# A seven-product group for the third row group of the first two down-projection blocks, in three of the four quarters of both MLPs

## The chip, the cores and the metric

The kernel runs on one core of one Trainium2 chip. The metric is the device time of one execution in microseconds (us); lower is better. Before the change the median of three runs is 1988.44 us (1988.22 to 1989.09).

## What is computed

A decoder trunk of two layers on 256 tokens (two tiles of 128) with a stream of width 2048, all in float32: differential attention and an MLP, then a shared latent K/V, latent attention and a second MLP. The change touches the MLPs alone. Their width is 8192:

```
def sq_relu_mlp(h, w_up, w_down):
    return jnp.square(jax.nn.relu(h @ w_up)) @ w_down
...
        x = x + sq_relu_mlp(rms_norm(x, mlp_norm_g[l]), w_up[l], w_down[l])
```

## The kernel before

**Three products for one.** Every float32 product is made of three: an operand is split into a high part (rounded to the format in which TensorE multiplies) and a low part (the rest), and high x high, high x low and low x high are summed in PSUM. Activations are split once (`opA` holds the normalised input, `opB` the hidden activations). Weights are split as they stream in: SyncE loads quads of 512 rows x 512 columns (4 chunks of 128 rows, 1 MB) into the four slots of `raw`, ScalarE copies two chunks at a time to `whi` (`split` of ScalarE, L1080), VectorE subtracts the copy from `raw` into `wlo` (`split` of VectorE, L1672), and TensorE runs the twelve 512-column matmuls of these two chunks (`half_tok`, L595 to L597: 2 chunks x 2 token tiles x 3). Such a piece is called a half here; a quad has two, a block of 2048 rows x 512 columns eight. `whi` and `wlo` are rings of four halves: ScalarE may write a half when TensorE has done the one four places earlier, so VectorE can be at most some four halves ahead.

**The MLP.** The hidden width is worked in four quarters of 2048 (`QUARTERS`). In a quarter the up-projection makes four hidden blocks of 512 columns (j = 0 to 3), each squared, turned (a transpose of 32x32 blocks on VectorE, four DMAs from `o_sb` to `prob` by SyncE's `move_quads`) and split into `opB`. Then the down-projection multiplies them by four column blocks of `w_down` (j = 0 to 3), each with four row groups r = 0 to 3 of 512 rows; row group r needs hidden block r. Blocks 0 and 1 are `first_down`, blocks 2 and 3 are `pair` (in the last quarter: plain blocks). TensorE's order in `first_down` is `DOWN_ORDER`, pairs (j, r), so that the last hidden block is used late:

```
DOWN_ORDER = ((0, 0), (0, 1), (0, 2), (1, 0), (0, 3), (1, 1), (1, 2), (1, 3))
```

**Seven products instead of eight.** Two quads of the same rows in two column blocks, times two token tiles, make a 2x2 by 2x2 product of blocks (256 rows x 512 columns x 128 tokens each). Plain, it costs four halves, 48 matmuls. `seven` makes it of seven products of six matmuls (L828 to L830), 42 in all, in the order `FORMS`: B22, T1, B21, B11, T2, T3, T4. It needs sums of activations (`form_sums`, `form_low` of VectorE; `form_high` of ScalarE), four sums of weights (VectorE, L2199, L2202, L2209, L2213), and each of the seven weight operands split on its own: four through the ring (L2188), three (T1, B11, T3) through `extra_hi`/`extra_lo` (L2182), which has two places, so T3 may be written only when TensorE has done T1 of the same group. Four of the products go to more than one output: they are summed in four PSUM banks of their own (`side`), copied out by ScalarE, mixed by four VectorE operations (`combine`, L2105), and added to the outputs. The up-projection uses one group per pair of blocks, `pair` two (row groups 2 and 3), which share the `side` banks, one copy and one `combine`. `down_add` (L2251, two operations of 128x1024) adds the mixed shares of `pair` to the residual stream `xs`, inside the group of the next up-projection (`up_pair`, after its first weight sum). `add_scaled` (L2136) adds the accumulators.

VectorE's and ScalarE's orders are written out by hand: `body`, `pair` and `up_pair` say after which split which other step comes. Each engine executes in its own order.

## Time and profile before

| | us |
|---|---|
| median of three runs | 1988.44 |
| the profiled execution, its own time | 1988.36 |
| its span, first to last instruction | 1986.6 |
| TensorE matmuls busy | 1977.4 (9128 matmuls) |
| TensorE weight loads busy | 1651.8 |
| VectorE busy | 1582.4 |
| ScalarE busy | 1161.1 |
| DMA, mean rate | 204 GB/s |

The chain of work that ended last is TensorE for 97% of the span and VectorE for 1%. Matmuls are pipelined: the recorded length of one (0.39 us) overlaps the next, and what counts is the distance between two starts. The same holds for VectorE, whose records of 1.22 us start 1.14 us apart when nothing is waited for. A bracket at the end of a timeline row is idle time of the engine before the instruction, and what ended it.

### The profile page before, as it was taken

What the parts mean: (1) busy time and instruction counts of PE and PEld (TensorE: products, weight loads), DVE (VectorE), ACT (ScalarE), POOL (GpSimd) and SP (SyncE); (2) the same over time, 40 slices, a digit from 0 to 9 for tenths busy, and PEclk for the clock granted to TensorE, in tenths of its full rate; (3) what the DMA queues carried; (4) which work ended last, traced back from release to release, by engine and by line L of the source; (5) the groups of instructions that cost most, each with busy time, mean ns of one, the idle gap of its engine ahead of it and who ended that gap; (6) DMA issues with size and microseconds to landing.
All of it is one profiled execution on the core that took longest, in us unless ns stands there. A gap on an engine that the chain in (4) does not pass through costs nothing.

```text
span 1986.6 us, 24882 instructions
## 1 busy us (share of the span) xinstructions
PE 1977.4 (100%) x9128; PEld 1651.8 (83%) x9128; DVE 1582.4 (80%) x1931; ACT 1161.1 (58%) x1481; POOL 13.2 (1%) x21
## 2 busy tenths in 40 slices
PE   9999999999999999999999999999999999999998
PEld 8888888888888888888888998888888888888887
DVE  7789996678888798788866787667798788889865
ACT  6555555556566456556656665556456556655653
POOL 0000000000000000000000000000000000000000
PEclk9999999999999999999999999999999999999999
DMA  8655546666566557656766554676557656656663
GB/s 307 212 170 189 182 157 216 225 194 234 190 215 223 191 200 241 220 190 202 242 212 195 143 152 151 223 229 223 181 194 240 223 199 212 227 186 212 212 240 106
DMA packets 265924, 405.26 MB, mean 204 GB/s; under 512 B 18416, under 2 KB 88432, under 8 KB 265840
## 3 DMA queue, kind: packets, MB, share of 16 engines
q1 hardware_dynamic: 251920, 395.82, 60.0%
q10 hardware_dynamic: 13920, 8.39, 1.5%
q8 instruction: 44, 0.72, 0.1%
q14 instruction: 40, 0.33, 0.0%
HBM read 379.00 MB, written 2.10 MB: 192 GB/s over the span
## 4 chain that ended last, share of the span: by engine, by line
PE 97%; issue 2%; DVE 1%; ACT 0%; POOL 0%; POOLq 0%; DVEq 0%; ACTq 0%
PE acc L595 24%; PE acc L597 24%; PE acc L596 24%; PE side L829 2%; PE side L830 2%; PE side L828 2%; PE acc L828 2%; PE acc L830 2%; PE acc L615 2%; PE acc L616 2%; PE acc L617 2%; PE acc L829 2%; PE acc L933 1%; PE acc L934 1%; PE acc L935 1%
## 5 line engine op out<-in xcount | busy, mean ns | idle before, releaser
L1672 DVE TENSOR_TENSOR wlo<-raw,whi 128x1024 fp32r<-128x1024 f32 (+1 forms) x596 | 709.7, 1206 | 214.7 <-ACT whi L1080 212.8
L1080 ACT ACTIVATE whi<-raw 128x1024 fp32r<-128x1024 f32 (+1 forms) x596 | 614.0, 1046 | 431.6 <-PE acc L597 360.4
L595 PE MATMUL acc<-whi,opB 128*128 128x512 f32 x1104 | 431.2, 391 | 0.1
L597 PE MATMUL acc<-whi,opB 128*128 128x512 f32 x1104 | 430.1, 390 | 0.0
L596 PE MATMUL acc<-wlo,opB 128*128 128x512 f32 x1104 | 429.9, 389 | 0.0
L595 PE MATMUL acc<-whi,opA 128*128 128x512 f32 (+2 forms) x1072 | 415.0, 387 | 0.0
L597 PE MATMUL acc<-whi,opA 128*128 128x512 f32 (+2 forms) x1072 | 414.2, 386 | 0.0
L596 PE MATMUL acc<-wlo,opA 128*128 128x512 f32 (+2 forms) x1072 | 414.1, 386 | 0.0
L597 PEld LDWEIGHTS acc<-whi,opB 128*128 128x128 f32 x1104 | 207.3, 188 | 43.2
L595 PEld LDWEIGHTS acc<-whi,opB 128*128 128x128 f32 x1104 | 207.4, 188 | 42.7 <-DVE wlo L1672 0.3
L596 PEld LDWEIGHTS acc<-wlo,opB 128*128 128x128 f32 x1104 | 207.4, 188 | 42.5
L597 PEld LDWEIGHTS acc<-whi,opA 128*128 128x128 f32 x1072 | 201.4, 188 | 40.0
L596 PEld LDWEIGHTS acc<-wlo,opA 128*128 128x128 f32 x1072 | 201.5, 188 | 39.8
L595 PEld LDWEIGHTS acc<-whi,opA 128*128 128x128 f32 x1072 | 201.5, 188 | 39.8
L1405 ACT ACTIVATE whi<-raw 128x1024 fp32r<-128x1024 f32 x78 | 82.9, 1063 | 96.5 <-DVE raw L2209 49.0
L1401 ACT ACTIVATE extra_hi<-raw 128x1024 fp32r<-128x1024 f32 x52 | 54.7, 1052 | 84.0 <-PE side L830 84.0
L2188 DVE TENSOR_TENSOR wlo<-raw,whi 128x1024 fp32r<-128x1024 f32 x78 | 95.1, 1219 | 0.0
L2182 DVE TENSOR_TENSOR extra_lo<-raw,extra_hi 128x1024 fp32r<-128x1024 f32 x52 | 63.6, 1222 | 23.1 <-ACT extra_hi L1401 23.1
L2087 DVE STREAM_TRANSPOSE o_sb<-junk 128x1024 f32<-128x1024 f32 x32 | 39.8, 1243 | 44.8 <-ACT junk L1359 44.8
L615 PE MATMUL acc<-whi,opA 128*128 128x512 f32 x184 | 72.0, 391 | 0.3 <-DVE wlo L1672 0.2
L616 PE MATMUL acc<-wlo,opA 128*128 128x512 f32 x184 | 71.7, 390 | 0.0
L617 PE MATMUL acc<-whi,opA 128*128 128x512 f32 x184 | 71.7, 389 | 0.0
(379 smaller groups left out, 2383.3 us busy)
## 6 DMA issues: line engine op xcount, KB each, us to landing
raw<-in_w_up SPq DMA_DIRECT2D x128, 1024.0 KB, 5.5
raw<-in_w_down SPq DMA_DIRECT2D x128, 1024.0 KB, 5.1
raw<-in_a_w_qkv SPq DMA_DIRECT2D x44, 1024.0 KB, 5.1
raw<-in_a_w_o SPq DMA_DIRECT2D x16, 1024.0 KB, 5.1
prob<-o_sb SPq DMA_DIRECT2D x128, 128.0 KB, 2.6
raw<-in_b_w_o SPq DMA_DIRECT2D x16, 1024.0 KB, 5.0
raw<-in_w_ukv SPq DMA_DIRECT2D x32, 256.0 KB, 4.2
prob<-o_sb ACTq DMA_DIRECT2D x48, 128.0 KB, 4.3
```

The lines of the kernel that those rows point to most:

```text
L595: mm(o, a_hi, w_hi, start=start, stop=False)
L596: mm(o, a_hi, w_lo, start=False, stop=False)
L597: done = mm(o, a_lo, w_hi, start=False, stop=last and c == chunks - 1)
L615: mm(o, a_hi, whi[:, place, :], start=start, stop=False)
L616: mm(o, a_hi, wlo[:, place, :], start=False, stop=False)
L617: done = mm(o, a_lo, whi[:, place, :], start=False, stop=end)
L828: mm(o, a_hi, hi[:, place + c, :], start=first and c == 0, stop=False)
L829: mm(o, a_hi, lo[:, place + c, :], start=False, stop=False)
L1080: done = fn(whi[:, place:place + ch, 0:n], raw[:, r, c0:c0 + ch, 0:n], ACT.Copy)
L1405: fn(whi[:, 2 * (hf % 4):2 * (hf % 4) + 2, :], source[f], ACT.Copy).then_inc(hi_ready, 1)
L1672: done = tt_(wlo[:, place:place + ch, 0:n], raw[:, r, c0:c0 + ch, 0:n], whi[:, place:place + ch, 0:n].bitcast(F32), ALU.subtract)
L2188: tt_(wlo[:, places, :], src, whi[:, places, :].bitcast(F32), ALU.subtract).then_inc(lo_ready, 1)
```

## The change

In quarters 0 to 2 of both MLPs row group 2 of down blocks 0 and 1 becomes a seven-product group of its own kind, "first". TensorE's order in `first_down` is now (0,0), (0,1), (1,0), (1,1), the group, (0,3), (1,3). Its four shares are copied by ScalarE at the end of `first_down`, combined by VectorE in `pair` between the two groups there, and added to `xs[:, :, 0:1024]` by a `down_add` in `pair`. The combine and `down_add` of `pair`'s own shares move on into the next `up_pair`. The activation sums for row group 2 are made straight from the turned hidden block (no more rebuilt from `opB`), so that the move of the next hidden block waits for them. TensorE's hardware loop over the quarters is written out. What only renumbers groups, shares and places is left out:

```diff
-DOWN_ORDER = ((0, 0), (0, 1), (0, 2), (1, 0), (0, 3), (1, 1), (1, 2), (1, 3))
+DOWN_FIRST = ((0, 0), (0, 1), (1, 0), (1, 1))
+DOWN_LAST = ((0, 3), (1, 3))
+LAST_DOWN = ((0, 0), (0, 1), (0, 2), (1, 0), (0, 3), (1, 1), (1, 2), (1, 3))
...
+def groups_of(l):
+
+    made = [("up", l, 0, 1)]
+    for q in range(QUARTERS - 1):
+        made += [("first", l, q), ("down", l, q, 0), ("down", l, q, 1), ("up", l, q + 1, 0), ("up", l, q + 1, 1)]
+    return made
...
@@ SyncE @@
+                    if j == JB - 1 and q < QUARTERS - 1:
+                        sp.wait_ge(form_step, 4 * (FORM_SETS * l + 2 * q + 1) + 4)
...
-                    for k, (j, r) in enumerate(DOWN_ORDER):
+                    order = DOWN_FIRST + ((0, 2), (1, 2)) + DOWN_LAST
+                    if q == QUARTERS - 1:
+                        order = LAST_DOWN
+                    for k, (j, r) in enumerate(order):
...
-                        quad(b + i // 4, i % 4, src, later=int(i == 6))
+                        quad(b + i // 4, i % 4, src, later=int(i in (0, 6)))
...
@@ TensorE @@
+                    for k, (j, r) in enumerate(DOWN_FIRST):
+                        plain_quad(k, j, r)
+                    pe.wait_ge(hid_lo, n + 6)
+                    shares_free(SHARE["first", l, q])
+                    pe.wait_ge(form_lo, FORM_SETS * l + 2 * q + 2)
+                    seven(GROUP["first", l, q], b + 1, 0, opB, 8, [forms[0][:, i] for i in range(2)], None, True, SHARED)
+                    for k, (j, r) in enumerate(DOWN_LAST):
+                        plain_quad(6 + k, j, r)
 
-                with pe.Fori(0, QUARTERS - 1) as q:
+                for q in range(QUARTERS - 1):
                     first_down(q)
...
@@ ScalarE @@
+                def copy_shared():
+                    for k in range(4):
+                        fn(down_shared[k], side[k], ACT.Copy).then_inc(shared_copied, 1)
...
+                def first_down(q):
+
+                    b = B_MLP[l] + 2 * JB * q + JB
+                    split(b, 3)
+                    square_second(q, 1)
+                    split(b, 4)
+                    hid_high(q, JB - 2)
+                    split(b, 5)
+                    split(b, 6)
+                    down_forms(q, 0)
+                    split(b, 7)
+                    seven(GROUP["first", l, q], b + 1, 0, (0, b + 1), (1, b + 1), {"B11": lambda: hid_high(q, JB - 1)})
+                    for hf in range(4, 8):
+                        split(b + 1, hf)
+                        if hf == 5:
+                            down_forms(q, 1)
+                    copy_shared()
+                    for hf in range(3):
+                        split(b + 2, hf)
...
                     split(b + 2, 0)
                     split(b + 2, 1)
-                    for k in range(4):
-                        fn(down_shared[k], side[k], ACT.Copy).then_inc(shared_copied, 1)
+                    act.wait_ge(shared_added, 2 * DOWN_SHARE["first", l, q] + 2)
+                    copy_shared()
                     split(b + 2, 2)
...
@@ VectorE @@
+                def down_add(key, c0):
+
+                    dve.wait_ge(shared_sums, 4 * SHARE[key] + 4)
+                    for s in range(2):
+                        dve.wait_ge(drained[s], 2 * (u[s] + U_QUARTER * key[2] + U_UP + c0 // 2 + 1))
+                    for t, both in enumerate((junk[:].rearrange("p a n -> p (a n)"), o_sb[:].rearrange("p a t n -> p (a t n)"))):
+                        stt(out=xs[:, t, NB * c0:NB * c0 + 2 * NB], in0=both, scalar=rs[:, 2 * l + 1, t:t + 1],
+                            in1=xs[:, t, NB * c0:NB * c0 + 2 * NB], op0=ALU.mult, op1=ALU.add).then_inc(shared_added, 1)
+
+                def first_down(q):
+
+                    b, key = B_MLP[l] + 2 * JB * q + JB, ("first", l, q)
+                    uses = [u[s] + U_QUARTER * q + U_UP for s in range(2)]
+                    split(b, 3)
+                    up_turn(q, JB - 1)
+                    split(b, 4)
+                    hid_low(q, JB - 2)
+                    form_sums(sqT, down_set(q, 0))
+                    split(b, 5)
+
+                    def after_first():
+                        split(b, 6)
+                        form_low(down_form(0), down_set(q, 0))
+
+                    seven(GROUP[key], b + 1, 0, (0, b + 1), (1, b + 1), 8 * b + 3,
+                          {"first sum": after_first, "second sum": lambda: split(b, 7), "B11": lambda: hid_low(q, JB - 1)})
...
-                    seven(down_groups(l, q, 0), 1, b, 4, (2, b), (3, b), 8 * b + 3, {"first sum": lambda: split(b, 3)})
+                    seven(GROUP["down", l, q, 0], b, 4, (2, b), (3, b), 8 * b + 3, {"first sum": lambda: split(b, 3)})
+                    combine(SHARE["first", l, q], down_shared)
                     split(b + 1, 0)
-                    seven(down_groups(l, q, 1), 2, b + 1, 2, (1, b + 1), (2, b + 1), 8 * b + 8,
+                    seven(GROUP["down", l, q, 1], b + 1, 2, (1, b + 1), (2, b + 1), 8 * b + 8,
                           {"first sum": lambda: split(b + 1, 1)})
                     split(b + 1, 6)
+                    down_add(("first", l, q), 0)
                     split(b + 1, 7)
...
                     for hf in range(3):
                         split(b + 2, hf)
-                    combine(down_shares(l, q), down_shared)
                     add_scaled(b + 1, 0, 2 * uses[0], slice(3 * NB, 4 * NB))
...
                         if follows == "down":
-                            down_add(q - 1)
+                            combine(SHARE["down", l, q - 1, 0], down_shared)
...
-                    if follows != "down":
+                    if follows == "down":
+                        after["T4"] = lambda: down_add(("down", l, q - 1, 0), 2)
+                    else:
                         after["T4"] = lambda: hid_low(q, 2 * i - 1)
```

**How the order moves.** Three places on VectorE. The first is `pair`, from T3 and T4 of its first group to the middle of its second. Before (L2182 and L2188 are the low parts of a group, L1672 that of a plain half, L2199, L2202, L2209, L2213 the weight sums):

```order
L2182 TENSOR_TENSOR extra_lo<-raw,extra_hi 128x1024
L2188 TENSOR_TENSOR wlo<-attn_both,whi 128x1024
L1672 TENSOR_TENSOR wlo<-raw,whi 128x1024
L2199 TENSOR_TENSOR attn_both<-raw 128x1024
L1672 TENSOR_TENSOR wlo<-raw,whi 128x1024
L2202 TENSOR_TENSOR raw<-raw 128x1024
L2188 TENSOR_TENSOR wlo<-raw,whi 128x1024
L2182 TENSOR_TENSOR extra_lo<-attn_both,extra_hi 128x1024
L2209 TENSOR_TENSOR raw<-attn_both,raw 128x1024
```

And with the change (L2211 and L2217 are the low parts of a group, L1705 that of a half, L2138 is `combine`):

```order
L2211 TENSOR_TENSOR extra_lo<-raw,extra_hi 128x1024
L2217 TENSOR_TENSOR wlo<-attn_both,whi 128x1024
L2138 TENSOR_TENSOR o_sb<-o_sb,junk 128x512
L2138 TENSOR_TENSOR junk<-junk,o_sb 128x512
L2138 TENSOR_TENSOR o_sb<-o_sb 128x512
L2138 TENSOR_TENSOR o_sb<-junk,o_sb 128x512
L1705 TENSOR_TENSOR wlo<-raw,whi 128x1024
L2228 TENSOR_TENSOR attn_both<-raw 128x1024
L1705 TENSOR_TENSOR wlo<-raw,whi 128x1024
L2231 TENSOR_TENSOR raw<-raw 128x1024
L2217 TENSOR_TENSOR wlo<-raw,whi 128x1024
```

Four operations have come in between the low part of T4 and that of the next half. The second place is `up_pair` after a `pair`, from T3 of its group on. Before:

```order
L2182 TENSOR_TENSOR extra_lo<-raw,extra_hi 128x1024
L2188 TENSOR_TENSOR wlo<-attn_both,whi 128x1024
L1672 TENSOR_TENSOR wlo<-raw,whi 128x1024 x4
L2105 TENSOR_TENSOR junk<-junk 128x512
L2105 TENSOR_TENSOR attn_both<-attn_both,junk 128x512
```

With the change (L2259 is `down_add`):

```order
L2211 TENSOR_TENSOR extra_lo<-raw,extra_hi 128x1024
L2217 TENSOR_TENSOR wlo<-attn_both,whi 128x1024
L2259 SCALAR_TENSOR_TENSOR xs<-junk,rs,xs 128x1024
L2259 SCALAR_TENSOR_TENSOR xs<-o_sb,rs,xs 128x1024
L1705 TENSOR_TENSOR wlo<-raw,whi 128x1024 x4
```

Two operations stand now ahead of the four halves that follow the group. The third place is the new group in `first_down`, with the change, from the low part of hidden block 2 on (L2128 is `hid_low`, L2180 to L2185 `form_sums`, L2190 `form_low`):

```order
L2128 TENSOR_TENSOR opB<-prob,opB 128x4x256
L2180 TENSOR_TENSOR qk_first<-prob 128x256
L2181 TENSOR_TENSOR qk_first<-prob 128x256
L2183 TENSOR_TENSOR qk_first<-prob,qk_first 128x256
L2185 TENSOR_TENSOR qk_first<-prob,qk_first 128x256
L1705 TENSOR_TENSOR wlo<-raw,whi 128x1024
L2228 TENSOR_TENSOR attn_both<-raw 128x1024
L1705 TENSOR_TENSOR wlo<-raw,whi 128x1024
L2190 TENSOR_TENSOR v_hl<-qk_first,v_hl 128x1024
L2231 TENSOR_TENSOR raw<-raw 128x1024
L1705 TENSOR_TENSOR wlo<-raw,whi 128x1024
L2217 TENSOR_TENSOR wlo<-raw,whi 128x1024
```

Before, three plain low parts stood behind the first of these rows, and the form sums came later.

## Rows read from the trace of the kernel before

**Rows 1.** The page: busy time of each engine.
```profile
PE 1977.4 (100%) x9128; PEld 1651.8 (83%) x9128; DVE 1582.4 (80%) x1931; ACT 1161.1 (58%) x1481; POOL 13.2 (1%) x21
```
**Rows 2.** The waits of TensorE: who released it, us, times, longest.
```profile
PE side L648 <- DVE junk L1827: 1.1, 1, 1.1
...
PE acc L615 <- DVE wlo L1672: 0.2, 1, 0.2
```
**Rows 3.** Stages first_down, pair: us; PE, PEld, DVE, ACT, POOL busy; granted clock, DMA.
```profile
465.60:509.13 43.53, 43.53 (x193) 36.05 (x192) 31.68 (x35) 23.83 (x23) 0.00 (x0) 1.00 0.66 220
509.13:552.99 43.86, 43.86 (x193) 36.02 (x192) 39.62 (x38) 25.23 (x27) 0.00 (x0) 1.00 0.61 203
```
**Rows 4.** Timeline, TensorE, that quarter: start us, us, line, operation.
```profile
509.13 0.39 PE L595 MATMUL acc<-whi,opB 128*128 128x512 f32 x1
...
520.02 0.40 PE L828 MATMUL acc<-whi,v_hl 128*128 128x512 f32 x1
...
529.75 0.39 PE L595 MATMUL acc<-whi,opB 128*128 128x512 f32 x1
...
539.39 0.39 PE L828 MATMUL side<-extra_hi,opB 128*128 128x512 f32 x1
...
576.45 0.39 PE L595 MATMUL acc<-whi,opA 128*128 128x512 f32 x1
```
**Rows 5.** Timeline, VectorE, pair: T3 and T4 of its first group onward.
```profile
524.17 1.23 DVE L2182 TENSOR_TENSOR extra_lo<-raw,extra_hi 128x1024 fp32r<-128x1024 f32 x1 [2.07 <-ACT extra_hi L1401]
525.31 1.22 DVE L2188 TENSOR_TENSOR wlo<-attn_both,whi 128x1024 fp32r<-128x1024 f32 x1
526.44 1.22 DVE L1672 TENSOR_TENSOR wlo<-raw,whi 128x1024 fp32r<-128x1024 f32 x1
...
536.66 1.22 DVE L2182 TENSOR_TENSOR extra_lo<-raw,extra_hi 128x1024 fp32r<-128x1024 f32 x1
...
539.35 1.22 DVE L2182 TENSOR_TENSOR extra_lo<-raw,extra_hi 128x1024 fp32r<-128x1024 f32 x1 [0.33 <-ACT extra_hi L1401]
```
**Rows 6.** Timeline, VectorE, end of pair: the combine.
```profile
550.33 0.68 DVE L2105 TENSOR_TENSOR o_sb<-o_sb,junk 128x512 f32<-128x512 f32 x1
...
553.11 1.40 DVE L2136 SCALAR_TENSOR_TENSOR xs<-acc,rs,xs 128x512 f32<-128x512 f32 x2
```
**Rows 7.** Timeline, VectorE, up_pair: down_add, and behind T3 of its group.
```profile
556.70 1.28 DVE L2251 SCALAR_TENSOR_TENSOR xs<-junk,rs,xs 128x1024 f32<-128x1024 f32 x1
...
559.09 1.22 DVE L1672 TENSOR_TENSOR wlo<-raw,whi 128x1024 fp32r<-128x1024 f32 x1
...
570.86 1.23 DVE L2182 TENSOR_TENSOR extra_lo<-raw,extra_hi 128x1024 fp32r<-128x1024 f32 x1 [0.33 <-ACT extra_hi L1401]
...
573.14 3.49 DVE L1672 TENSOR_TENSOR wlo<-raw,whi 128x1024 fp32r<-128x1024 f32 x3
```
**Rows 8.** Timeline, VectorE then TensorE: a matmul kept waiting, first block.
```profile
22.54 1.23 DVE L1672 TENSOR_TENSOR wlo<-raw,whi 128x1024 fp32r<-128x1024 f32 x1 [0.68 <-ACT whi L1080]
...
23.25 0.40 PE L617 MATMUL acc<-whi,opA 128*128 128x512 f32 x1
23.82 0.50 PE L615 MATMUL acc<-whi,opA 128*128 128x512 f32 x1 [0.17 <-DVE wlo L1672]
24.16 0.39 PE L616 MATMUL acc<-wlo,opA 128*128 128x512 f32 x1
```
**Rows 9.** Timeline, VectorE, first_down of that quarter.
```profile
472.41 1.23 DVE L2095 TENSOR_TENSOR opB<-prob,opB 128x1024 fp32r<-128x1024 f32 x1
...
481.89 0.42 DVE L2145 TENSOR_TENSOR qk_first<-prob 128x256 f32<-128x256 f32 x1
...
483.35 1.22 DVE L1672 TENSOR_TENSOR wlo<-raw,whi 128x1024 fp32r<-128x1024 f32 x1
```
**Rows 10.** Timeline, SyncE's queue; the page: issue to landing, us.
```profile
464.93 3.70 SPq L394 DMA_DIRECT2D raw<-in_w_down  x2
...
raw<-in_w_down SPq DMA_DIRECT2D x128, 1024.0 KB, 5.1
```

More of the change, by code:

```diff
@@ L452, in move_quads @@
                     sp.wait_ge(sqT_done, n + 1)
[L453 removed]
+                    if n:
                         sp.wait_ge(hid_lo, 2 * n)
+                    if j == JB - 1 and q < QUARTERS - 1:
+                        sp.wait_ge(form_step, 4 * (FORM_SETS * l + 2 * q + 1) + 4)
                     for a in range(4):
@@ L802, in mlp, with seven @@
                 u = U_MLP[l]
-                def seven(group, at, b, hf0, buf, c0, made, uses, opens, closes):
+                def seven(group, b, hf0, buf, c0, made, uses, opens, closes):
                     act11, act12 = ([[buf[:, c0 + 2 * k + c, i, 0:P] for i in range(2)] for c in range(2)]
@@ L813, in seven @@
                     for f in FORMS:
-                        shares = f in ("T1", "B11", "T2", "T3")
+                        shares = f in SHARED
                         if f in IN_EXTRA:
-                            pe.wait_ge(extra_lo_ready, len(IN_EXTRA) * group + IN_EXTRA.index(f) + 1)
-                            hi, lo, place = extra_hi, extra_lo, extra_place(l, at, f)
+                            e = extra_number(group, f)
+                            pe.wait_ge(extra_lo_ready, e + 1)
+                            hi, lo, place = extra_hi, extra_lo, 2 * (e % 2)
                         else:
@@ L821, in seven @@
                             hi, lo, place = whi, wlo, 2 * (hf % 4)
-                        first, last = opens and (shares or f == "B22"), closes and f != "B22"
-                        if opens and f == "B22":
+                        first, last = opens and (shares or f == "B22" and uses is not None), f in closes
+                        if opens and f == "B22" and uses is not None:
                             wait_bank(0, uses, 0)
@@ L833, in shares_free @@
                 def shares_free(share):
-                    if not (isinstance(share, int) and share == 0):
+                    if share:
                         pe.wait_ge(shared_copied, 4 * share)
@@ L1396, in seven @@
                         if f in IN_EXTRA:
-                            e = len(IN_EXTRA) * group + IN_EXTRA.index(f)
-                            if not (isinstance(e, int) and e < 2):
+                            e = extra_number(group, f)
+                            if e >= 2:
                                 act.wait_ge(pe_extra, e - 1)
-                            place = extra_place(l, at, f)
+                            place = 2 * (e % 2)
                             fn(extra_hi[:, place:place + 2, :], source[f], ACT.Copy).then_inc(extra_hi_ready, 1)
@@ L2204, in seven @@
                         after["second sum"]()
-                    low("B22", group, at, b, hf0, b22)
-                    low("T1", group, at, b, hf0, w_sum)
+                    low("B22", group, b, hf0, b22)
+                    low("T1", group, b, hf0, w_sum)
                     dve.wait_ge(w_summed, n + 2)
@@ L2209, in seven @@
                     tt_(b22, w_sum, b22, ALU.add).then_inc(w_summed, 1)
-                    low("B21", group, at, b, hf0, b21)
+                    low("B21", group, b, hf0, b21)
                     dve.wait_ge(w_summed, n + 3)
@@ L2213, in seven @@
                     tt_(w_sum, b22, b21, ALU.add).then_inc(w_summed, 1)
-                    low("B11", group, at, b, hf0, b11)
-                    low("T2", group, at, b, hf0, b22)
-                    low("T3", group, at, b, hf0, b12)
+                    low("B11", group, b, hf0, b11)
+                    if "B11" in after:
+                        after["B11"]()
+                    low("T2", group, b, hf0, b22)
+                    low("T3", group, b, hf0, b12)
                     dve.wait_ge(w_summed, n + 4)
-                    low("T4", group, at, b, hf0, w_sum)
+                    low("T4", group, b, hf0, w_sum)
```

139 lines of the change are left out of this document (65 added, 74 removed).

## The prediction, made before the changed kernel was run

> **What bounds the kernel now.** The page comes first: TensorE is busy for 1977.4 of 1986.6 us, VectorE for 1582.4 [rows 1]. TensorE's list of waits says how full that is: the longest is 1.1 us at the very start, and the only wait for a low part of weights is 0.2 us [rows 2]. In the stages that the change touches TensorE has no idle time at all (43.53 of 43.53 us in `first_down`, 43.86 of 43.86 in `pair`), at a granted clock of 1.00 [rows 3]. So each matmul taken away is worth its full distance to the next, and the time that TensorE is kept waiting for VectorE is a loss at full price. The hardware loop over the quarters runs through these stages without a gap, so writing it out gains nothing.
>
> VectorE's 80% is a mean over stages. In `first_down` it is busy 31.7 of 43.5 us, in `pair`, with two groups, 39.6 of 43.9 [rows 3]: in `pair` four us are left, and the question is where in the order they lie. That is read from the timeline: for each low part its end, and the start of the first matmul that uses it. The difference is called margin here.
>
> **What the change gives.** Four plain halves take TensorE from 509.13 to 520.02, 10.89 us; a group takes it from 520.02 to 529.75, 9.73 us [rows 4]. Six matmuls fewer are worth 1.16 us and not 6 x 0.227, since a group's matmuls start a little further apart. Six groups (three quarters, two layers): 6 x 1.16 = **7.0 us gained**.
>
> **What it adds.** Per quarter VectorE gets three more low parts and four weight sums, and loses the rebuilding of `act_whole`: six operations more in `first_down`, at 1.135 us from start to start (524.17, 525.31, 526.44) [rows 5] 6.8 us. It also gets a `combine`, 2.78 us from its first operation to the next instruction (550.33 to 553.11) [rows 6], and a `down_add`, 2.39 us (556.70 to 559.09) [rows 7]. ScalarE gets three copies of 1.05 us and four of about half that; it is busy 23.8 of 43.5 us there [rows 3] and hides them.
>
> *In `first_down`: nothing, I think.* `hid_low` starts at 472.41 and the next operation 1.135 us later; four form sums take 1.46 us (481.89 to 483.35) [rows 9]; so the low part behind them starts at 475.0, the group's first sum at 476.15, and after four operations more the low part of B22 at 481.8. TensorE, which starts the stage at 465.6 and takes 2.72 us a half (10.89 / 4), comes to B22 after eight halves, at 487.4: margin 4.3. Ten operations later, with the second `hid_low` among them, T2's low part ends at 491.0 and is wanted at 492.9. T3 cannot be early in any group: its place is freed by TensorE's T1, ScalarE then copies and VectorE starts, as at 524.17 after 2.07 us idle [rows 5]. It ends at 525.40 and is wanted two products before 529.75, at about 526.96: margin 1.6. The new group meets this same pattern. Behind it form sums and `form_low` lie between halves that come every 2.72 us and cost 1.14. The cover is the full ring, and it is gone if a wait of over 1.6 us arises. The first sum now needs slot 1 early: its load is the second of the two that span 464.93 to 468.63, issued at some 468.3, and lands 5.1 us later [rows 10], at 473.4, against 476.15. The wait of SyncE for the form sums delays its queue by 1.46 us and holds only loads that are wanted 20 us later.
>
> *In `pair`: two stalls that are one.* The `combine` of the new shares comes straight behind T4 of the first group, while VectorE has just been held by T3. Before, the low part of the next half starts at 526.44 [rows 5], ends at 527.66, and is wanted at 529.75 [rows 4]: margin 2.09. With 2.78 us put ahead it ends at 530.44, 0.69 late. From there VectorE runs without a pause to T3 of the second group (539.35, 0.33 idle before it) [rows 5], so all in between is 2.78 us later. The worst of it is B11: low part at 536.66 [rows 5], ended 537.88, wanted at 539.39 [rows 4], margin 1.51; late by 1.27. The first stall counts toward the second; together TensorE loses 1.27. A restart costs on top: in the first block a low part ended at 22.54 + 1.23 = 23.77, the matmul was due at 23.25 + 0.23 = 23.48, and the one behind it started at 24.16 where 23.71 was due [rows 8]: 0.45 lost for 0.29 late, 0.16 more. So **1.43 us per quarter**. The `down_add` behind the half after T4 then puts the last half of `pair` at 548.74, wanted at 547.67 + 1.43 = 549.1: it just fits.
>
> *In `up_pair`: a third.* The old `combine` takes the place of the old `down_add` after the first weight sum (2.78 for 2.39; TensorE is 1.4 us later by then, so it fits), and `down_add` now stands behind T4. T3 is again held to TensorE's T1 (570.86, 0.33 idle), the next half's low part at 573.14 [rows 7], ended 574.36, is wanted at 576.45 [rows 4]: margin 2.09 against 2.39. Late by 0.30, with the restart **0.46 us**. Since T3 hangs on TensorE itself, an earlier stall does not soften this one.
>
> The added instructions have rows of their own kind, so only these prices have bounds: the restart costs between 0 and the 0.34 us that the first matmul took to the next (23.82 to 24.16) [rows 8]; 0.16 is taken, as what was lost there. That makes the stalls 1.57 to 2.25 us, 1.89 taken.
>
> *VectorE's pace.* Its rows are 1.22 us long and start 1.135 us apart [rows 5], and I count starts. The Trainium skill (VectorE: DVE Perf Modes, The DRAIN you can't avoid) says that the next operation does not start until the pipeline of the one before is empty; read so, lengths would count: `down_add` 2 x 1.28 = 2.56 us, the third stall 0.63 and the sum 1.0 us higher. These rows disagree with it for operations in a row, and starts stay.
>
> **The sum.** Per quarter -1.16 + 1.43 + 0.46 = +0.73 us; six of them +4.4 us. The profiled execution took 1988.36 us by its own time (span 1986.6), 0.08 under the median of the runs, which I neglect: **1992.8 us**. With the bounds of the restart 1990.8 to 1994.9. A measurement of this kernel tells about 0.2%, 4.0 us, from no change; the line to slower is 1992.4, just under the forecast.
>
> **The rivals.**
> - *The stalls don't come* (faster). VectorE has 400 us idle in all, and 2.07 us just before T3 of `pair`'s first group [rows 5]. If the added work found such room, the 7.0 us would stay: 1981.4 us. It would take a `combine` that fits into the margin of 2.09 us; but the order puts it behind that idle time, and its 2.78 us are measured [rows 6]. 7%.
> - *Only the stall in `pair` comes.* `down_add` is late by 0.30 alone; if T3 is freed a little earlier or the ring hides it, the sum is 6 x (1.43 - 1.16) = +1.6: 1990.0 us. 13%.
> - *More stalls than I count.* `first_down` is close to full (38.5 of 42.4 us of VectorE), the last half of `pair` has 0.36 us left, and slot 1 has 2.8 us. One more stall of 0.5 to 1.4 us per quarter adds 3 to 8 us: about 1998 us. For: hand-counted margins leave things out. Against: each new wait has cover above. 15%.
> - *VectorE advances by lengths.* 1993.8 us; the starts in rows 5 speak against. 3%.
> - That the change doesn't do what it says is out: the order shows 36 matmuls fewer.
>
> **How the numbers follow.** The forecast itself has 62%. Spread over 1990.8 to 1994.9 it lies for about four parts in ten below 1992.4. Faster: 7%. Within 0.2%: 13% and 0.4 x 62%, 38%. Slower: the rest, 55%. The range goes from 1989.8 (the second rival in) to 1998.0 (most of the third in), leaving out the fast case and the far end of the third.
>
> **What would show it.** TensorE 9092 matmuls; VectorE busy some 76 us more (6 x (6 x 1.22 + 2.75 + 2.56)). In TensorE's waits, new: in each of six `pair`s one for `wlo` of the half behind the first group (the stretch from group start to that half 0.85 us longer than 9.73) and one for `extra_lo` of B11 (0.6 more), in each `up_pair` behind it one for `wlo` (0.46). `first_down` without a wait, 42.4 us long. It is wrong if TensorE waits in `first_down`, or if the half behind the first group starts 9.73 us after it.

## The result and the profile after

| | before | after |
|---|---|---|
| median of four runs, us | 1988.41 (1988.22 to 1989.09) | 2002.35 (2000.84 to 2003.65) |
| ratio after to before, 95% interval | | 1.0067 [1.0055, 1.0080] |
| the profiled execution, its own time | 1988.36 | 2000.84 |
| its span | 1986.6 | 1998.9 |

The change makes the kernel 13.9 us slower. The forecast was 1992.8 us with a range from 1989.8 to 1998.0: slower came out as predicted, by how much did not. The profiled execution of after is the fastest of its four runs; it carries 12.3 us of the difference in its span.

The page gives, beside [rows 1], the busy times. TensorE has the 36 matmuls less, and VectorE 64.4 us more, where some 76 were predicted; I had added record lengths for the 72 operations, and by starts it would have been 6 x (6.8 + 2.78 + 2.39) = 72. The lengths of all records do add up to 75.4 us more; busy time counts the overlap of two records once, and in after more of them follow one another without idle time.

```profile
PE 1977.9 (99%) x9092; PEld 1643.2 (82%) x9092; DVE 1646.8 (82%) x2003; ACT 1186.4 (59%) x1523; POOL 13.2 (1%) x21
```

TensorE's waits after (who released it, us, times, longest), where [rows 2] had 0.2 us for weights:

```profile
PE acc L590 <- DVE wlo L1705: 9.9, 16, 1.7
PE side L824 <- DVE extra_lo L2211: 1.6, 6, 0.3
PE side L643 <- DVE junk L1860: 1.1, 1, 1.1
```

The six waits for `extra_lo` are the ones predicted for B11. By the prediction there should have been 12 for `wlo`; the list has 16, and the starts of all matmuls show 18, three in each of the six quarters. The windows of after are `first_down`, which answers to the first of [rows 3], and what follows up to 595 us (us; PE, PEld, DVE, ACT, POOL busy; clock, DMA share, GB/s):

```profile
465.70:508.11 42.41, 42.41 (x187) 34.97 (x186) 37.79 (x41) 28.10 (x30) 0.00 (x0) 1.00 0.66 218
508.11:550.00 41.89, 41.03 (x178) 33.03 (x177) 39.51 (x38) 24.10 (x26) 0.00 (x0) 1.00 0.54 177
550.00:595.00 45.00, 43.84 (x192) 35.48 (x191) 40.08 (x40) 24.44 (x25) 0.00 (x0) 1.00 0.69 216
```

`first_down` takes 42.41 us instead of 43.53, without a wait. TensorE is idle only behind it, at four places. In its timeline each shows as a start that comes late, and a next one that is late a little more:

```profile
528.50 0.40 PE L826 MATMUL acc<-whi,opB 128*128 128x512 f32 x1
529.48 0.49 PE L590 MATMUL acc<-whi,opB 128*128 128x512 f32 x1 [0.58 <-DVE wlo L1705]
529.81 0.40 PE L591 MATMUL acc<-wlo,opB 128*128 128x512 f32 x1
...
539.02 0.40 PE L826 MATMUL acc<-whi,opB 128*128 128x512 f32 x1
539.70 0.50 PE L824 MATMUL side<-extra_hi,opB 128*128 128x512 f32 x1 [0.28 <-DVE extra_lo L2211]
540.03 0.40 PE L825 MATMUL side<-extra_lo,opB 128*128 128x512 f32 x1
...
561.46 0.39 PE L592 MATMUL acc<-whi,opA 128*128 128x512 f32 x1
562.52 0.51 PE L590 MATMUL acc<-whi,opA 128*128 128x512 f32 x1 [0.67 <-DVE wlo L1705]
562.86 0.40 PE L591 MATMUL acc<-wlo,opA 128*128 128x512 f32 x1
...
577.64 0.40 PE L826 MATMUL acc<-whi,opA 128*128 128x512 f32 x1
578.53 0.50 PE L590 MATMUL acc<-whi,opA 128*128 128x512 f32 x1 [0.49 <-DVE wlo L1705]
578.87 0.39 PE L591 MATMUL acc<-wlo,opA 128*128 128x512 f32 x1
```

The loss at such a place is the two distances between starts less the usual ones (0.23 each): at 562.52 it is 1.06 + 0.34 - 2 x 0.23 = 0.94 us. Done so for all six quarters that have the new group:

| stall | place | predicted, us a quarter | measured | six quarters |
|---|---|---|---|---|
| 1 and 2 | `pair`: the half behind the first group; B11 of the second | 1.43 | 1.38 to 1.42 | 8.4 |
| 3 | next `up_pair`: half 4 of its first block, one half ahead of the last plain one | none | 0.28 to 1.94 | 5.1 |
| 4 | next `up_pair`: the half behind T4 | 0.46 | 0.77 to 0.82 | 4.7 |

That is 18.2 us against 11.3 predicted. The gain is 1.12 us a quarter by the two windows of `first_down`, 6.7 us for six, so the stalls leave +11.5 of the 12.3 us in the spans. 0.1 us is there before the first changed stage (465.70 against 465.60 us); the other 0.7 us I can't place.

Stall 3 is the one to explain. VectorE's timeline of after, at 554 to 562 us and behind T3:

```profile
553.67 1.22 DVE L1705 TENSOR_TENSOR wlo<-raw,whi 128x1024 fp32r<-128x1024 f32 x1
557.32 1.23 DVE L2228 TENSOR_TENSOR attn_both<-raw 128x1024 f32<-128x1024 f32 x1 [2.43 <-issue]
558.46 0.69 DVE L2138 TENSOR_TENSOR o_sb<-o_sb,junk 128x512 f32<-128x512 f32 x1
...
561.25 1.22 DVE L1705 TENSOR_TENSOR wlo<-raw,whi 128x1024 fp32r<-128x1024 f32 x1
...
572.60 1.22 DVE L2211 TENSOR_TENSOR extra_lo<-raw,extra_hi 128x1024 fp32r<-128x1024 f32 x1
...
574.87 1.27 DVE L2259 SCALAR_TENSOR_TENSOR xs<-junk,rs,xs 128x1024 f32<-128x1024 f32 x1
...
577.26 4.62 DVE L1705 TENSOR_TENSOR wlo<-raw,whi 128x1024 fp32r<-128x1024 f32 x4
```

VectorE stands idle for 2.43 us before the first weight sum of the group, and only then come the `combine` and the low part at 561.25, for which TensorE waits. "issue" names no releaser. The sum reads slot 0 of the next block's `raw`. SyncE (SPq is its queue) issues the load of it as follows, in after and then in before, where the sum ran at once:

```profile
551.33 0.37 SPq L384 DMA_DIRECT2D raw<-in_w_up  x1
```

```profile
548.85 0.37 SPq L394 DMA_DIRECT2D raw<-in_w_up  x1
...
555.56 1.22 DVE L2199 TENSOR_TENSOR attn_both<-raw 128x1024 f32<-128x1024 f32 x1
```

From issue to sum it is 5.99 us after, 6.71 before. By VectorE's own order the sum could have started at 554.89, 0.67 us earlier than before; by the load, which is issued 2.48 us later, it could not. When a load landed is in the trace too. These two rows are the same load in before and then in after; the last number is the time from its issue to its landing:

```profile
raw<-in_w_up SPq DMA_DIRECT2D x1, 1024.0 KB, 5.1
```

```profile
raw<-in_w_up SPq DMA_DIRECT2D x1, 1024.0 KB, 5.9
```

In before the load is there at 553.9, 1.6 us ahead of the sum (1.1 to 1.7 in the six quarters). In after it lands at 557.2 and the sum starts within 0.1 us, and so it is in all six quarters. So the sum waits for this load. It comes late for two reasons: it is issued 2.48 us later, against 1.6 us of slack, and it takes 0.8 us longer.

SyncE issues it when half 1 of the block before has its low part, and that low part is later because the new `down_add` stands ahead of it in `pair`. Half 1 is the second low part of the last row, in after and then in before; it ends at 551.30 and at 548.82, 0.03 us ahead of each issue:

```profile
544.10 1.28 DVE L2259 SCALAR_TENSOR_TENSOR xs<-junk,rs,xs 128x1024 f32<-128x1024 f32 x1
545.30 1.28 DVE L2259 SCALAR_TENSOR_TENSOR xs<-o_sb,rs,xs 128x1024 f32<-128x1024 f32 x1
...
548.95 3.49 DVE L1705 TENSOR_TENSOR wlo<-raw,whi 128x1024 fp32r<-128x1024 f32 x3
```

```profile
546.47 2.35 DVE L1672 TENSOR_TENSOR wlo<-raw,whi 128x1024 fp32r<-128x1024 f32 x2
```

VectorE's list of waits says how often it waits before such a sum, before and then after:

```profile
DVE attn_both L2199 <- issue: 15.7, 6, 2.8
```

```profile
DVE attn_both L2228 <- issue: 30.6, 12, 3.4
```

Six more waits and 14.9 us more; the six new ones themselves are 1.79 to 3.40 us long, 14.0 together. That the sum waits for the load is read from the trace; that TensorE's stall comes from it, and not from the work that VectorE has besides, was still to be shown. Two theories went to the experiments. **Load theory**: stall 3 comes from the late load. **Work theory**: VectorE just has too much to do between the groups, and the load doesn't matter.

### The profile page after: what moved, and what is told of

Same layout as the page of the kernel before. It is cut to its first block, busy times and chain, and to the rows that moved or that the text cites. A ratio compares the mean times of both kernels' runs of the same rounds, so it can differ in the third digit from the quotient of the medians.

```text
span 1998.9 us, 24494 instructions
## 1 busy us (share of the span) xinstructions
PE 1977.9 (99%) x9092; PEld 1643.2 (82%) x9092; DVE 1646.8 (82%) x2003; ACT 1186.4 (59%) x1523; POOL 13.2 (1%) x21
## 4 chain that ended last, share of the span: by engine, by line
PE 81%; DVE 13%; issue 5%; DMA 1%; ACT 1%; POOL 0%; POOLq 0%; DVEq 0%; ACTq 0%
PE acc L590 21%; PE acc L592 20%; PE acc L591 20%; DVE wlo L1705 3%; DVE wlo L2217 3%; PE acc L610 2%; PE acc L611 2%; PE acc L612 2%; PE side L824 2%; PE side L826 2%; PE side L825 2%; DVE xs L2259 1%; DVE extra_lo L2211 1%; PE acc L824 1%; PE acc L826 1%
## 5 line engine op out<-in xcount | busy, mean ns | idle before, releaser
L1705 DVE TENSOR_TENSOR wlo<-raw,whi 128x1024 fp32r<-128x1024 f32 x572 | 679.5, 1205 | 158.1 <-ACT whi L1090 156.6
L1090 ACT ACTIVATE whi<-raw 128x1024 fp32r<-128x1024 f32 x572 | 586.7, 1045 | 354.0 <-PE acc L592 283.0
L590 PE MATMUL acc<-whi,opB 128*128 128x512 f32 x1008 | 394.7, 392 | 3.5 <-DVE wlo L1705 3.5
L592 PE MATMUL acc<-whi,opB 128*128 128x512 f32 x1008 | 393.0, 390 | 0.0
L591 PE MATMUL acc<-wlo,opB 128*128 128x512 f32 x1008 | 392.8, 390 | 0.0
L590 PEld LDWEIGHTS acc<-whi,opB 128*128 128x128 f32 x1008 | 189.4, 188 | 44.9 <-DVE wlo L1705 6.4
L592 PEld LDWEIGHTS acc<-whi,opB 128*128 128x128 f32 x1008 | 189.4, 188 | 39.5
L591 PEld LDWEIGHTS acc<-wlo,opB 128*128 128x128 f32 x1008 | 189.4, 188 | 38.6
L1419 ACT ACTIVATE whi<-raw 128x1024 fp32r<-128x1024 f32 x96 | 101.9, 1061 | 123.3 <-DVE raw L2238 61.4
L1415 ACT ACTIVATE extra_hi<-raw 128x1024 fp32r<-128x1024 f32 x64 | 67.3, 1052 | 92.0 <-PE side L826 92.0
L2217 DVE TENSOR_TENSOR wlo<-raw,whi 128x1024 fp32r<-128x1024 f32 x96 | 117.0, 1218 | 0.0
L2211 DVE TENSOR_TENSOR extra_lo<-raw,extra_hi 128x1024 fp32r<-128x1024 f32 x64 | 78.1, 1221 | 22.2 <-ACT extra_hi L1415 22.2
```

Source lines behind the costliest of these rows:

```text
L590: mm(o, a_hi, w_hi, start=start, stop=False)
L591: mm(o, a_hi, w_lo, start=False, stop=False)
L592: done = mm(o, a_lo, w_hi, start=False, stop=last and c == chunks - 1)
L1090: done = fn(whi[:, place:place + ch, 0:n], raw[:, r, c0:c0 + ch, 0:n], ACT.Copy)
L1415: fn(extra_hi[:, place:place + 2, :], source[f], ACT.Copy).then_inc(extra_hi_ready, 1)
L1419: fn(whi[:, 2 * (hf % 4):2 * (hf % 4) + 2, :], source[f], ACT.Copy).then_inc(hi_ready, 1)
```

## The experiments

In each the kernel before ran on the same chip; its medians were 1989.16 us beside the first four runs, 1988.43 beside the next four and 1988.95 beside the last two.

**The loop written out (e1).** The kernel before, with one line of the change:

```diff
-                with pe.Fori(0, QUARTERS - 1) as q:
+                for q in range(QUARTERS - 1):
```

> The kernel before with TensorE's hardware loop over the quarters written out, and nothing else. My theory (all of the change's loss is TensorE kept waiting for VectorE's low parts): no difference, within 1 us of the kernel before (about 1988.4 us), no idle time of TensorE in the MLP stages. Rival (the 2.5 to 3 us per quarter that are lost come in part from the written-out instruction stream, 1.10 instead of 0.72 MB of it): several us slower.

Measured: 1989.63 us, ratio 1.0003 [0.9993, 1.0012]; no stall in these stages, span 1987.7. Writing out the loop costs and gives nothing that can be told, as predicted. Its span is 1.1 us over that of before, but 0.85 us of this is there at 68 us, ahead of the MLPs.

**The first combine earlier (e2).** The changed kernel, with the `combine` taken out of `pair` and put into `first_down`, where [rows 3] had left room:

```diff
@@ VectorE, first_down @@
                     add_scaled(None, 1, 2 * uses[1], slice(0, NB))
+                    combine(SHARE["first", l, q], down_shared)
                     split(b + 2, 1)
@@ VectorE, pair @@
-                    combine(SHARE["first", l, q], down_shared)
```

> The changed kernel, with the combine of the new group's shares moved from behind the first group of pair to the end of first_down, behind the first add_scaled, where VectorE has 0.9 us of idle time and 2.1 more ahead of T3. My theory: the two stalls in pair (0.85 and 0.55 us a quarter) go; the load of the next up-projection's first slot is issued over 1 us earlier, so that the third stall shrinks from 0.86 to 0 to 0.3 us a quarter; the fourth, behind T4 of up_pair, stays at 0.46. Sum: 1988.4 - 7.0 + 2.8 + 0 to 1.8, 1984 to 1986 us. Rival (VectorE's total work is what counts, not its place): no change, about 2002 us.

Measured: 1994.35 us, ratio 1.0025 [1.0015, 1.0036], 8 us above the range of the expectation. Stalls 1 and 2 are gone (in one quarter of six 1.0 us is left, in two others 0.1). That confirms their cause, the `combine` behind T4. Against the expectation stall 3 stays (0.41 to 1.68 us, 6.5 in all), and so does stall 4 (0.77 to 0.81). The load is issued 1.26 us earlier than in after (550.07), as expected, but without stalls 1 and 2 TensorE is some 1.4 us earlier too, and nothing is won. VectorE now has more room ahead of `up_pair` and still waits before the first sum:

```profile
DVE attn_both L2228 <- issue: 31.0, 12, 3.2
```

So stall 3 has nothing to do with stalls 1 and 2, and this speaks against the work theory. A VectorE that is further ahead also meets a load in a place where neither before nor after waits: the first sum of `pair`'s second group waits for `w_down` in each of the six quarters, 8.8 us in all. The longest of these waits is in the quarter in which 1.0 us of stall is left:

```profile
699.48 1.23 DVE L2228 TENSOR_TENSOR attn_both<-raw 128x1024 f32<-128x1024 f32 x1 [2.32 <-DMA raw<-in_w_down]
```

**The addition a half later (e3).** The changed kernel; `down_add` of the first shares moved behind half 1 of the up block, whose low part frees the slot, so that the load could be issued earlier.

```diff
@@ VectorE, pair @@
-                    down_add(("first", l, q), 0)
...
                         split(b + 2, hf)
+                        if hf == 1:
+                            down_add(("first", l, q), 0)
```

> The changed kernel, with the down_add of the new shares moved some 3.5 us later, behind the second half of the next block, on whose low part the load into slot 0 waits. VectorE's work and everything else are the same. My theory (the third stall is a late load): the low part comes 2 us earlier, so does the load; the third stall (0.86 us a quarter) goes and the fourth falls from 0.79 to 0.46, while both stalls in pair stay: about 7 us less, 1995 us, and the runs spread less than the 2.8 us of the changed kernel's. Rival (the third stall is VectorE out of time, by the work put ahead): no change or slower, 2002 us or more.

Measured: 2008.06 us, ratio 1.0095 [1.0078, 1.0112], slower than the change itself. The edit made a wait of its own: ScalarE's copies of `pair`'s shares overwrite what `down_add` reads and must wait for it, and ScalarE's next copies of weights stand behind them. ScalarE's row, then VectorE's:

```profile
554.48 1.09 ACT L1396 ACTIVATE junk<-side 128x512 f32<-128x512 f32 x2 [4.98 <-DVE xs L2259]
```

```profile
557.52 1.23 DVE L1705 TENSOR_TENSOR wlo<-raw,whi 128x1024 fp32r<-128x1024 f32 x1 [3.08 <-ACT whi L1090]
```

Stall 3 becomes 1.9 us for another reason. It tells nothing on the load; e5 repeats it without that wait.

**Both pieces of new work in other places (e4).** `combine` in `first_down` as in e2; the new `down_add` cut in two, its first tile behind T2 in `pair`'s first group, where VectorE waits for T3's place anyway, its second behind the last half of that block; `pair`'s own `combine` and `down_add` back at their places of before.

```diff
@@ VectorE, pair @@
-                    seven(..., {"first sum": lambda: split(b, 3)})
-                    combine(SHARE["first", l, q], down_shared)
+                    seven(..., {"first sum": lambda: split(b, 3), "T2": lambda: down_add(("first", l, q), 0, (0,))})
...
+                    down_add(("first", l, q), 0, (1,))
...
+                    combine(SHARE["down", l, q, 0], down_shared)
@@ VectorE, up_pair @@
-                            combine(SHARE["down", l, q - 1, 0], down_shared)
+                            down_add(("down", l, q - 1, 0), 2)
```

> The changed kernel with all its additions put where VectorE has room: combine of the new shares at the end of first_down, their down_add in two parts, one ahead of T3 in pair's first group (where VectorE idles), one behind the last half of pair; the other shares' combine and down_add back where they were before the change. My theory: no stall is left, all 7.0 us of the gain show: 1981.4 us. Rival (VectorE has not enough room in these stages wherever the work is put): it stays above 1988 us.

Measured: **1983.49 us** (1982.04 to 1985.19), ratio 0.9973 [0.9963, 0.9982], faster than before and after. That is 5.7 us under before, where the gain of the six groups was to be 7.0, and 2.1 us over the 1981.4 expected. VectorE does all the work of the change. TensorE's waits:

```profile
PE side L643 <- DVE junk L1860: 1.1, 1, 1.1
PE acc L610 <- DVE wlo L1705: 0.2, 1, 0.2
```

No stall of the four is left. Its span is 1980.6, 7.1 us under that of e1 with as few stalls (6.1 by the medians); 0.4 us of the 7.1 lies ahead of the MLPs, so the six groups give some 6.7. VectorE has the room; the change put the work where there was none.

**e3 without the wait of ScalarE (e5).** As e3, and `pair`'s copies of shares moved into the next `up_pair`:

```diff
@@ ScalarE @@
-                    act.wait_ge(shared_added, 2 * DOWN_SHARE["first", l, q] + 2)
-                    copy_shared()
...
+                    if after == "down":
+                        act.wait_ge(shared_added, 2 * DOWN_SHARE["first", l, q - 1] + 2)
+                        copy_shared()
```

> The changed kernel with the shares' addition of the first group a half later in the last blocks of the quarter (as in e3) and ScalarE's copying of the pair's own shares moved out of ScalarE's way, into the next up-projection pair, so that nothing on ScalarE waits for the addition. Load theory (the third stall is VectorE's first weight sum waiting for a load that was issued late, because the low part of half 1 that frees its slot is late): that low part is again about two us earlier, the load with it, the third stall goes, and the fourth falls back to about 0.46 us; the two stalls in the last down blocks stay (1.4 us a quarter). 2002 - 5 - 2 = about 1995 us (1993 to 1996). Rival (VectorE simply has too much work between the two groups, wherever it lies): the third stall stays at 0.8 to 1 us and the time at 2001 to 2004 us.

Measured: 1997.9 us (1995.08 to 1998.79), ratio 1.0040 [1.0026, 1.0055], between the two expectations. The load is issued at 550.12, counted from stall 1 2.05 us earlier than in after (19.80 against 21.85 us), nearly as meant; but from its issue to the sum it now takes 7.33 us instead of 5.99, so the sum starts only 0.7 us earlier. The idle time before the sum falls from 2.43 to 1.38 us, and stall 3 from 5.1 to 1.7 us in the six quarters (none in two of them). Stall 4 hardly falls (0.61 to 0.82). Lateness of the sum and stall 3 fall together, as the load theory says; the size that it gave, which took the load's duration as fixed, is wrong.

**The load alone (e6).** The changed kernel; no computing engine's work or order is touched. The one load of slot 0 is cut in two, the first half of it issued as soon as its own chunks are free, and the first sum waits for that half alone.

```diff
@@ SyncE @@
+                        if after_pair and k == 4:
+                            sp.wait_ge(lo_ready, 8 * (b + 1) - 7)
+                            sp.dma_start(raw[:, 0, 0:2, :], src[:, 0:2]).then_inc(half_up, 16)
+                            sp.wait_ge(lo_ready, 8 * (b + 1) - 6)
+                            sp.dma_start(raw[:, 0, 2:4, :], src[:, 2:4]).then_inc(raw_ready[0], 16)
@@ VectorE, seven @@
+                    if halves:
+                        dve.wait_ge(half_up, 16 * halves)
```

> The changed kernel with one 1 MB load cut in two: the load of the first weight slot of the second block of an up-projection pair that follows the down blocks; its first two chunks are loaded one half earlier, and the first weight sum of the group waits for these alone. VectorE's and ScalarE's work and order are untouched. Load theory: the first weight sum starts without idle time (2.4 us idle now), the third stall goes, the fourth falls to about 0.5 us, the other two stay: about 1995 us (1993 to 1997). Rival (VectorE's work, not the load): the same stalls, 2001 to 2004 us.

Measured: 1994.2 us (1993.29 to 1994.95), ratio 1.0026 [1.0016, 1.0037]. Counted from stall 1 (530.33 here, 529.48 in after) the first half is issued 1.14 us earlier than the whole load was, and the sum starts 1.19 us earlier. The idle time before the sum, which the expectation had at nothing, falls to 1.25 us:

```profile
556.98 1.23 DVE L2238 TENSOR_TENSOR attn_both<-raw 128x1024 f32<-128x1024 f32 x1 [1.25 <-issue]
```

TensorE runs through the place of stall 3 in all six quarters, and stall 4 falls to 0.46 to 0.60. The waits:

```profile
PE acc L597 <- DVE wlo L1712: 4.9, 12, 0.6
PE side L831 <- DVE extra_lo L2218: 1.6, 6, 0.3
```

Twelve and six, as the prediction had it, 11.4 us of stalls where it had 11.3. This is the changed kernel about as I had forecast it: 5.8 us over before against the +4.4 of the sum.

**Stall 4 alone (e7).** The kernel before, with only `down_add` moved behind T4 of the next `up_pair`'s group (and `sum_first` waiting for it, which VectorE has always done by then):

```diff
-                        if follows == "down":
-                            down_add(q - 1)
...
+                    after["T4"] = (lambda: down_add(q - 1)) if follows == "down" else (lambda: hid_low(q, 2 * i - 1))
```

> The kernel before, with one move alone: the addition of the down shares to the stream goes from behind the first weight sum of the next up-projection pair to behind T4 of its group. This is the fourth stall by itself. By the hand count of the prediction the next low part is 0.30 us late and the matmuls lose 0.46 us, six times: +2.8 us, about 1992.0 us. If what it cost in the changed kernel (0.77 to 0.81 us) is a property of the move alone: +4.7 us, about 1993.9. If the move is free when nothing else is changed: 1989.2.

Measured: 1991.62 us (1990.96 to 1992.34), ratio 1.0014 [1.0005, 1.0024], 3.2 us. Six stalls of 0.46 or 0.47, nothing else. VectorE and TensorE:

```profile
571.55 1.22 DVE L2184 TENSOR_TENSOR extra_lo<-raw,extra_hi 128x1024 fp32r<-128x1024 f32 x1 [2.72 <-ACT extra_hi L1401]
...
576.22 4.63 DVE L1672 TENSOR_TENSOR wlo<-raw,whi 128x1024 fp32r<-128x1024 f32 x4
```

```profile
577.49 0.50 PE L595 MATMUL acc<-whi,opA 128*128 128x512 f32 x1 [0.19 <-DVE wlo L1672]
577.83 0.39 PE L596 MATMUL acc<-wlo,opA 128*128 128x512 f32 x1
```

The hand count of 0.46 is exact where T3 is held to TensorE (2.72 us idle ahead of it). In after T3 has no idle time ahead of it (572.60 above): VectorE is late from stall 3 on, and stall 4 grows to 0.79.

**e4 with the old places of the new work (e8).** `combine` back behind T4 of `pair`'s first group, the `down_add` whole behind that block's last half; the rest as e4.

```diff
@@ VectorE, pair, against e4 @@
+                    combine(SHARE["first", l, q], down_shared)
...
-                    down_add(("first", l, q), 0, (1,))
+                    down_add(("first", l, q), 0)
```

> The version e4 with the combine of the first group's shares put back behind T4 of the first group in the last down blocks, and the whole addition of these shares behind the last half there. Theory: stalls one and two come back (1.4 us a quarter, 8.4 in all); whether the third comes depends on how late the load of the first slot is issued, 0 to 0.5 us a quarter: 1991 to 1995 us. If the time in e4 was won only by moving the additions and not by the place of the combine: 1983 to 1986 us.

Measured: 1996.68 us (1996.4 to 1997.0), ratio 1.0039 [1.0025, 1.0053], 13.2 us over e4 and above the range of 1991 to 1995. Stalls 1 and 2 return with 8.3 us, and a stall at place 3 of 0.78 to 0.84 us, nearly the same in all quarters, where 0 to 0.5 was expected. Here the load has landed 0.3 to 0.9 us ahead of the first sum, which (558.57) follows the instruction before it without idle time; VectorE is late by its own work. So in this order the work theory holds for place 3, though not in after.

**The late load put into the kernel before (e9).** The opposite of e6: no new work, only SyncE held.

```diff
@@ SyncE, up_pair @@
+                        if after_pair and k == 4:
+                            sp.wait_ge(shared_sums, 4 * down_shares(l, q - 1) + 2)
```

> The kernel before, its computation and every engine's order unchanged; only SyncE, ahead of the load of the first weight slot of the next block in an up-projection pair behind the down blocks, also waits for the second of the combine's four operations. The load is then issued at about 551.8 instead of 548.85 us, 2.9 us later, as it is in the changed kernel (2.5 later). Load theory: VectorE's first weight sum starts 1.6 to 2.9 us later than at 555.56, the low part behind it is 0.65 to 1.9 us too late against its margin of about 1 us, so the third stall appears alone, 0.8 to 2.0 us, six times: 1993.5 to 2000 us. Rival (the stall came from VectorE's added work): no stall and 1988.4 us.

Measured: 1995.71 us (1995.31 to 1996.73), ratio 1.0034 [1.0021, 1.0046], 6.8 us. SyncE, VectorE, and TensorE's waits:

```profile
552.35 0.37 SPq L394 DMA_DIRECT2D raw<-in_w_up  x1
```

```profile
557.70 1.23 DVE L2201 TENSOR_TENSOR attn_both<-raw 128x1024 f32<-128x1024 f32 x1 [1.47 <-issue]
...
561.23 1.22 DVE L1674 TENSOR_TENSOR wlo<-raw,whi 128x1024 fp32r<-128x1024 f32 x1
```

```profile
PE acc L597 <- DVE wlo L1674: 5.4, 6, 1.4
```

Six stalls at place 3 and nowhere else, 0.74 to 1.72 us, 7.0 in all, within the range of the expectation. In five of the six quarters the sum starts within 0.1 us of the landing of the load, here too. With e6 this settles it: a load issued some 3 us late makes stall 3 without any added work, and in the order of after the added work doesn't make it once the load comes 1.1 us earlier.

**e2 and e6 together (e10).** The `combine` of e2 and the cut load of e6, no other edit.

> e2 and e6 together: the combine of the first group's shares already in the first down blocks, and the load cut in two. If the stalls have the two separate causes that e2 and e6 each took away, the first, second and third are gone and only the fourth stays at 0.46 us: 1994.35 - 6.5 - 2 = about 1986 us (1984.5 to 1988). If they are not independent (VectorE runs out of room in another place): 1990 us or more.

Measured: 1986.73 us (1985.76 to 1988.05), ratio 0.9990 [0.9980, 0.9999]. Left are six stalls at place 4, five of 0.46 or 0.47 and one of 0.80, and 1.0 us in scattered pieces, 4.2 in all. Each against the kernel before beside it, e2 takes 8.7 us off the 13.9 of the change and e6 8.2; together they take 16.2 of these 16.9. The causes are separate and add up.

## Why the prediction was right and wrong

- **The gain**: right, a little too large. 7.0 us predicted, 6.7 measured in `first_down`, and e4 shows as much.
- **`first_down` without a wait**: right, 42.41 us long where 42.4 was said. Of the rival "More stalls than I count" this part fell.
- **Stalls 1 and 2**: right in place, mechanism and size: 1.43 predicted, 1.38 to 1.42 measured, and 0.85 for the first alone. The restart's price of 0.16 us held: the distance behind a late start is 0.33 or 0.34 us where 0.23 is usual, and 0.05 us lie between low part and matmul.
- **Stall 3: the step that failed.** The prediction says of the old `combine` in `up_pair` that it "takes the place of the old `down_add` after the first weight sum (2.78 for 2.39; TensorE is 1.4 us later by then, so it fits)". That counts what VectorE does behind the sum and takes the sum's own start as given. The sum waits for a load, the load for SyncE, and SyncE for the low part of half 1 of the block before, which stands behind the `down_add` that the same prediction had just put into `pair`. I followed such a load once, for slot 1 in `first_down`, and not here. Ahead of the sum, before had a load issued at 548.85, landed at 553.9 and used at 555.56: 1.6 us of slack against 2.5 of delay, and in after the load took 0.8 us longer besides. The Trainium skill (DMA: Bandwidth & Descriptors, Bandwidth) gives 6.15 us as the transfer time of 1 MB, measured for loads issued from another engine; an estimate by that figure puts the sum of after at 551.33 + 6.15 = 557.5. The trace has 557.32 there, but this load took 5.1 to 5.7 us in the six quarters of before and 5.3 to 6.9 us in those of after, so one close match proves little. The term was put at nothing, and the stall cost 5.1 us by itself.
- **Stall 4**: right mechanism, mis-sized in after: 0.46 predicted, 0.79 measured. e7 shows that the 0.46 is the price of the move alone. "T3 is again held to TensorE's T1" did not hold in after, because VectorE ran late from the sum on. With the late load gone (e6) it is 0.46 to 0.60. So 1.7 of the 2.0 us missing here are stall 3's second cost.
- **The total**: 9.5 us over the forecast. Stall 3 is 5.1 of them and stall 4 2.0; stalls 1 and 2 took 0.2 less; the gain is 0.3 smaller; 0.8 us of the spans lies outside or isn't placed; and the median of after is 1.5 us over the profiled execution in which the stalls are counted.
- **The rivals**: the one that came true is the third, at 15%, one more stall in each quarter. Its range of 0.5 to 1.4 us was too narrow: 0.28 to 1.94. It named `first_down`, the last half of `pair` and slot 1 as the close places, and none of them was where the stall came. The ground given against it, that each new wait has cover above, was untrue for this wait. VectorE advances by starts, not lengths: e7's four operations from 571.55 to 576.22 take 4.67 us, the starts' count (1.14 + 1.14 + 2.39), where lengths would add up to 5.0.
- **The fast rival**, "the stalls don't come", was rightly put low for this order of the work. With the work in other places it is real: e4.

Stall 3 differs between quarters, from 0.28 to 1.94 us in after, though the order of all engines is the same in each. The trace says by what: the load's own time. From issue to sum and the stall behind it, quarter by quarter (us):

| | 1 | 2 | 3 | 4 | 5 | 6 |
|---|---|---|---|---|---|---|
| issue to sum, after | 5.99 | 5.78 | 6.96 | 5.47 | 5.35 | 5.82 |
| stall 3, after | 0.94 | 0.77 | 1.94 | 0.40 | 0.28 | 0.81 |

The difference is 5.0 to 5.1 us in each: for as long as a load takes beyond that, TensorE stands still. In e9 it is 4.6 us in five of six quarters. What stays open is why one load takes 5.3 us and another 6.9; that was not tried. That after's runs lie 2.8 us apart and e6's 1.7 fits a load time that varies, and is no proof.

## What to carry to other kernels

When work is put ahead of an instruction, follow what that instruction releases and not only what waits behind it: a low part that came 2.5 us later delayed the load issued on it, and over the six quarters that cost 5.1 us a stage further on, in a place where the engine stood idle for it. Before pricing added work as lost, look for stretches in which the engine waits for something anyway: the same operations in such places turned +13.9 us into -5.7. And to prove a cause, put it alone into the old kernel (e9) as well as taking it out of the new (e6); moving the work only (e3, e5) made new waits and told less.

## What was not expected of the hardware

A load's time from issue to use is no constant of these stages. The window from its issue to the sum, before and then after (us; PE, PEld, DVE, ACT, POOL busy; clock, DMA share, GB/s):

```profile
548.85:555.56 6.71, 6.71 (x31) 5.58 (x30) 6.27 (x8) 2.43 (x3) 0.00 (x0) 1.00 0.53 175
```

```profile
551.33:557.32 5.99, 5.99 (x28) 4.98 (x27) 3.56 (x5) 2.67 (x3) 0.00 (x0) 1.00 0.96 294
```

Before, the DMA engines are busy for 53% of it, after for 96%: with loads issued at 547.74, 551.33 and 554.92 the DMA engines had hardly a pause from the issue to the use. The load took 5.9 us to land, and 6.9 us in another quarter, against a median of 5.1 for `w_down` loads [rows 10]. How busy the DMA engines are doesn't give a load's time by itself: in e5 it was the longest of these, 7.33 us from issue to use, at 79%.

```profile
550.12:557.45 7.33, 7.33 (x34) 6.08 (x33) 5.95 (x7) 4.19 (x8) 0.00 (x0) 1.00 0.79 278
```

In e6 the 512 KB half that the sum needs took 5.94 us from issue to use, no less than the whole load in after: it was the earlier issue that helped. Why half the size did not come sooner was not tried.
